# Six plain output blocks become seven-product blocks, and the branch multiplications of the short convolution move ahead

## The chip, the cores and the metric

One core of one Trainium2 chip runs the whole program in one launch. The metric is the device time of that launch in microseconds (us). TensorE (PE) multiplies matrices, VectorE (DVE) and ScalarE (ACT) do elementwise work, GpSimd (POOL) here only adds and subtracts, and SyncE (SP) issues the weight loads. All data is float32.

## The reference

The program is a small network for 256 tokens of width 1024 (D). An MLA layer and an RG-LRU layer come first. Then come two hybrid layers, called L0 and L1 in the kernel, and a last layer, called C. Only the middle of those three layers matters here:

```python
# hybrid layer (L0, L1)
y_attn = dsa_attention(q, k, v, iq, ik, iw) @ w_attn_out
y_conf = silu(layer_norm(a, conf_ln_g, conf_ln_b)) @ w_conf_out
y_sc = (c_b * causal_dwconv(c_c * c_x, sc_conv_w)) @ w_sc_out
merged = gates[:, :, 0] * y_conf + gates[:, :, 1] * y_attn + gates[:, :, 2] * y_sc
x = x + merged @ w_o
# last layer (C)
a = ret @ w_ret_out
b = moba_attention(mq, mk, mv) @ w_moba_out
mix = sigmoid(ga) * a + sigmoid(gb) * b
x = x + mix @ w_o
```

Each of `w_attn_out`, `w_ret_out` and `w_o` is a 1024 by 1024 product on 256 tokens.

## The kernel before

**Stream of weights.** All weights come from one DRAM tensor in the order of use, in blocks of up to 1 MB. SP loads them in turn into a ring of two slots. A slot is loaded again when PE has signalled its last read of it and, for a seven-product block, when POOL has finished with it too.

**Plain block.** `halves` makes 256 output columns: two column tiles, each a sum over 8 k tiles of a 128x128 weight tile with 256 tokens. With `late=2` both column tiles are first summed over 6 k tiles, and then over the last two, whose activations come later.

**Seven-product block.** `fast_block` makes the same 256 columns by a Strassen-like form. Weights, tokens and the k tiles in pairs are cut in quarters, and seven products of four k pairs each (128x128x128) take the place of eight. The form needs three other things:
- POOL makes four mixed weight tiles (`mix`): a subtraction of 1024 columns (event mix1, line 1760), then two operations of 512 columns (mix2, line 1764, and mixed, line 1767). For the first block of some stages the subtraction is cut in two of 512 columns (lines 1755 and 1757). POOL takes the blocks strictly in their order. The mixed tiles lie in two buffers, so a block is mixed once the block two before it in that stage order has been multiplied.
- DVE makes four sums s1, s2, s4, s3 of the activations (`token_sums`, lines 2237, 2239, 2241, 2242). Each of the first three waits for the one before. PE multiplies two products of plain weights and activations first (called x0 and x2 here), then the third, x1, which needs s4. After those three the slot is released. Then come four products with mixed weights (y1, y2, y3, y0).
- DVE puts the seven results together after the last product (`unite`, lines 2218 to 2227), all with one operand or more in PSUM. That also frees the PSUM banks. The blocks take two banks each out of four, in rotation, so a block needs the bank pair of the one two before it.

**The stages around the change.** In a hybrid layer, after the convolutions, PE runs four plain blocks `cb` (q = 0 to 3). `branch_b(q)` on DVE (line 2410) multiplies their results into `ys` and frees their banks. DVE does between them the layer norm's factor, `short_conv(1)`, the operands `yc` of the `conf` branch with their sums, and the top-k rounds (`ranked`). Then eight attention heads go by (`heads` on DVE, `causal_heads` on PE). Beside each PE runs one seven-product block: `conf` 0 to 3, then `sc` 0 to 3. DVE normalises a head's probabilities (line 2108) for a transpose on PE.

After the heads come two output stages of four blocks each. `attn0` is plain (`late=2`), then `attn` 0 to 2 are seven-product blocks. DVE unites each, multiplies it by its gate (line 1811, result `tmp`) and adds it to `mg` (line 2510, both inputs in SBUF). Then `o0` is plain over `mg` (`late=2`), and `o` 0 to 2 are seven-product blocks whose results go into the residual `x_res`. The sums of `mg` for `o` are made in two parts: three k pairs after the second `attn` block and the last pair after the third. The next stage, `up0`, is plain and unchanged. Layer C has the same two stages under the names `ret0`, `ret`, `o0`, `o`, after the plain `moba` blocks. Its sums of `retn` come after the multiplication of the `moba` results.

Every engine works through its own list in program order, so what is written later on DVE waits for all that stands before it.

Of the kernel before, what the change touches and what calls it, by code (L numbers as in the profile page):

```python
# [20 lines left out]
P = 128  # L21
# [40 lines left out]
def stream_plan():  # L62
# [69 lines left out]
    pl("C.ret0", "w_ret_out_3", 0, 1, 1, 8, seq(0))  # L132
    fast("C.ret", "w_ret_out_3", 0, 3, 1, lambda it, q: 256 * it + 256)
    pl("C.o0", "w_o_3", 0, 1, 1, 8, seq(0))
    fast("C.o", "w_o_3", 0, 3, 1, lambda it, q: 256 * it + 256)
# [298 lines left out]
def write_program(nc, wstream, params, consts, tokens, out, counts):  # L434
# [3 lines left out]
    with ExitStack() as ctx:  # L438
# [268 lines left out]
        def _(pe):  # L707
# [112 lines left out]

            def of_tokens(buf):

                return lambda h, k, t: buf[:, 2 * k + h, P * t:P * t + P]
# [252 lines left out]
            for l in range(2):  # L1076
# [83 lines left out]
                def branch_block(h):  # L1160
# [7 lines left out]
                halves(L + "attn0", 0, 8, [P, P], lambda k: ya[:, k, :], S, ready=[(L + "ya", h) for h in range(8)], late=2)  # L1168
                fast_stage(F, "attn", 3, 1, of_tokens(ya), (F, "ya"), None)
                halves(L + "o0", 0, 8, [P, P], lambda k: mg[:, k, :], S,  # L1170
                       ready=[(L + "attn0", "m", 0, t) for t in range(2)] + [(F, "m", k // 2) for k in range(6)], late=2)
                fast_stage(F, "o", 3, 1, of_tokens(mg), (F, "mg"), None)
# [72 lines left out]
            for h in range(4):  # L1245
                pe.wait_ge(*e.at(("C.retn", h)))
            halves("C.ret0", 0, 8, [P, P], lambda k: retn[:, k, :], S)
            fast_stage("C", "ret", 3, 1, of_tokens(retn), ("C", "retn"), None)
            halves("C.o0", 0, 8, [P, P], lambda k: mg3[:, k, :], S,
                   ready=[("C.ret0", "m", 0, t) for t in range(2)] + [("C", "m", k // 2) for k in range(6)], late=2)  # L1250
            fast_stage("C", "o", 3, 1, of_tokens(mg3), ("C", "mg"), None)
# [12 lines left out]
        def _(act):  # L1264
# [173 lines left out]
            for l in range(2):  # L1438
# [128 lines left out]
                for part in ("attn", "o"):  # L1567
                    for it in range(3):
                        first_product((F, part, it, 0))
                boundary([(L + "o0", "x", j) for j in range(2)] + [(F, "o", "x", j // 2) for j in range(6)], L + "n2", x_res, f"norm2_g_2.{l}", xg_f)  # L1570
# [104 lines left out]
            for part in ("ret", "o"):  # L1675
                for it in range(3):
                    first_product(("C", part, it, 0))
            boundary([("C.o0", "x", j) for j in range(2)] + [("C", "o", "x", j // 2) for j in range(6)], "C.n2", x_res,
# [125 lines left out]
        def _(dve):  # L1804
# [427 lines left out]
            def sum_acts(sums, lo, hi, first=0):  # L2232
# [4 lines left out]
                dve.tensor_tensor(s1, a21, a22, ALU.add).then_inc(*e.step((sums, "sum", 0)))  # L2237
                dve.wait_ge(*e.at((sums, "sum", 0)))
                dve.tensor_tensor(s2, s1, a11, ALU.subtract).then_inc(*e.step((sums, "sum", 1)))  # L2239
                dve.wait_ge(*e.at((sums, "sum", 1)))  # L2240
                dve.tensor_tensor(s4, a12, s2, ALU.subtract).then_inc(*e.step((sums, "sum", 3)))  # L2241
                dve.tensor_tensor(s3, a11, a21, ALU.subtract).then_inc(*e.step((sums, "sum", 2)))  # L2242

            def token_sums(sums, a, first=0, n=4):

                both = a[:, 2 * first:2 * first + 2 * n, 0:S].rearrange("p (k two) t -> p k two t", two=2)
                sum_acts(sums, both[:, :, 0, :], both[:, :, 1, :], first)
# [16 lines left out]
            for l in range(2):  # L2264
# [181 lines left out]
                branch_b(1)  # L2446
# [14 lines left out]
                def short_sums(h):  # L2461

                    if h > 3:
# [32 lines left out]
                heads(L, probs, lambda t: sel[:, t, 0:P * (t + 1)], branches_part, short_sums)  # L2496
                branches_part(8)
                for h in range(8):
                    dve.wait_ge(*e.at((L + "ya", h)))
                token_sums((F, "ya"), ya)  # L2500
                gated_block(L + "attn0", 0, 8, False, sg, mg)
                for t in range(2):
                    dve.wait_ge(*e.at((L + "attn0", "m", 0, t)))
                for it in range(3):
                    tiles = slice(2 * it + 2, 2 * it + 4)
                    unite((F, "attn", it, 0), both_p, 0, (F, "y", it - 1) if it else (F, "branch", 8))
                    stt(tmp[:, 0:2, 0:S], sg[:, 2 * it + 10:2 * it + 12, :], 1.0, both_p, ALU.add,
# [7 lines left out]
                for t in range(2):  # L2515
                    key = (L + "o0", 0, t)
                    dve.wait_ge(*e.at(("pe", key)))
                    b = e.bank_of(key)
                    stt(x_res[:, t, :], psum[b][:, 0:S], 0.5, x_res[:, t, :], ALU.mult,
                        ALU.add).then_inc(*e.frees(key, (L + "o0", "x", t)))  # L2520
                for it in range(3):
                    unite((F, "o", it, 0), both_p, 0, (F, "o", "x", it - 1) if it else (F, "y", 2))
                    stt(x_res[:, 2 * it + 2:2 * it + 4, :], both_p, 0.5, x_res[:, 2 * it + 2:2 * it + 4, :], ALU.mult,
# [130 lines left out]
            heads("C.", probs3, lambda t: C(f"mask{t}"), beside=retention_part)  # L2654
            for h in range(8):
# [10 lines left out]
            for h in range(4):  # L2666
                dve.wait_ge(*e.at(("C.retn", h)))
            token_sums(("C", "retn"), retn)
            gated_block("C.ret0", 0, 0, False, gab, mg3)
            for t in range(2):  # L2670
                dve.wait_ge(*e.at(("C.ret0", "m", 0, t)))
            for it in range(3):
                tiles = slice(2 * it + 2, 2 * it + 4)
                unite(("C", "ret", it, 0), both_p, 0, *([("C", "y", it - 1)] if it else []))
                stt(tmp[:, 0:2, 0:S], gab[:, 2 * it + 2:2 * it + 4, :], 1.0, both_p, ALU.add,
# [4 lines left out]
                if it == 1:  # L2680
                    token_sums(("C", "mg"), mg3, 0, 3)
            token_sums(("C", "mg"), mg3, 3, 1)
            for t in range(2):
                key = ("C.o0", 0, t)
                dve.wait_ge(*e.at(("pe", key)))
                b = e.bank_of(key)
                stt(x_res[:, t, :], psum[b][:, 0:S], 0.5, x_res[:, t, :], ALU.mult,
                    ALU.add).then_inc(*e.frees(key, ("C.o0", "x", t)))
            for it in range(3):
                unite(("C", "o", it, 0), both_p, 0, ("C", "o", "x", it - 1) if it else ("C", "y", 2))  # L2690
                stt(x_res[:, 2 * it + 2:2 * it + 4, :], both_p, 0.5, x_res[:, 2 * it + 2:2 * it + 4, :], ALU.mult,
# [70 lines left out]
```

## Time and profile before

| what | value |
|---|---|
| median of 3 runs | 1975.94 us (1975.05 to 1976.07) |
| the profiled execution, its own time | 1974.15 us |
| its span in the profile | 1972.4 us |
| PE busy | 1956.2 us (99%) |
| DVE busy | 1170.5 us (59%) |
| POOL busy | 1105.9 us (56%) |
| ACT busy | 401.9 us (20%) |
| seven-product blocks changed or added | 6 plain blocks become seven-product ones |

The span runs from the first to the last instruction of one execution. The profile records each float32 multiplication of the program as two MATMUL instructions, so a plain block is 32 records and a seven-product block 56. The ends of matmuls are modelled, so lengths are best read from the starts.

### The profile page before, as it was taken

The numbers are of one execution on the slowest core, as the hardware profiler recorded it, in microseconds if no ns is written. First come the engines' busy times: TensorE is split into PE (matmuls) and PEld (weight loads), VectorE is DVE, ScalarE is ACT, GpSimd is POOL, SyncE is SP. The second block draws the span as 40 slices with busy tenths as digits, with TensorE's granted clock in tenths as the row PEclk, the third lists the DMA queues.
The fourth block names the chain that finished last, engine by engine and source line by source line (L and its number), as shares of the span: only waits on it lengthen the run. The fifth ranks groups of instructions, "written<-read, shape, count | busy, mean of one in ns | idle before, by whom it ended". The sixth has DMA issues, their size and how long they took to land. (4 is left out here: it accounts for less than half of the span.)

```text
span 1972.4 us, 37150 instructions
## 1 busy us (share of the span) xinstructions
PE 1956.2 (99%) x14762; PEld 1847.8 (94%) x14762; DVE 1170.5 (59%) x2996; ACT 401.9 (20%) x975; POOL 1105.9 (56%) x741
## 2 busy tenths in 40 slices
PE   9999999999999999999999999999999999999999
PEld 7788889999899999999999889999999999999998
DVE  4244535989966567524888976567713377454541
ACT  2241521111221222110111222222102025220000
POOL 1000038785174587758687154578776674348773
PEclk9999999999999999999999999999999999999999
DMA  5313445443444454545444343455444442445544
GB/s 211 134 43 133 149 152 181 156 169 131 137 153 144 150 174 170 166 156 171 165 158 170 121 149 143 146 175 169 166 160 161 138 149 95 142 150 172 171 161 139
DMA packets 44266, 299.74 MB, mean 152 GB/s; under 512 B 5440, under 2 KB 6592, under 8 KB 10176
## 3 DMA queue, kind: packets, MB, share of 16 engines
q1 hardware_dynamic: 42560, 295.42, 43.7%
q8 instruction: 118, 1.93, 0.4%
q10 hardware_dynamic: 1536, 1.97, 0.3%
q14 instruction: 52, 0.43, 0.1%
HBM read 294.35 MB, written 1.05 MB: 150 GB/s over the span
## 5 line engine op out<-in xcount | busy, mean ns | idle before, releaser
L714 PE MATMUL bank<-arena,ring 128*128 128x128 f32 (+2 forms) x3878 | 615.1, 312 | 1.3 <-ACT arena L1306 0.6
L714 PEld LDWEIGHTS bank<-arena,ring 128*128 128x128 f32 x3878 | 550.3, 191 | 45.9 <-ACT arena L1306 3.1
L714 PE MATMUL bank<-xn,ring 128*128 128x128 f32 (+3 forms) x3104 | 468.3, 306 | 4.6 <-DVE arena L2410 4.6
L714 PEld LDWEIGHTS bank<-xn,ring 128*128 128x128 f32 (+1 forms) x3104 | 424.3, 191 | 36.3 <-issue 9.8
L714 PE MATMUL bank<-arena 128*128 128x128 f32 (+5 forms) x2952 | 380.3, 284 | 0.0
L714 PEld LDWEIGHTS bank<-arena 128*128 128x128 f32 (+1 forms) x2952 | 353.9, 192 | 9.3 <-issue 1.5
L714 PE MATMUL bank<-arena,h_res 128*128 128x128 f32 x2696 | 322.1, 276 | 1.9 <-POOL h_res L1764 1.2
L714 PEld LDWEIGHTS bank<-arena,h_res 128*128 128x128 f32 x2696 | 310.4, 192 | 4.8 <-POOL h_res L1764 2.4
L1760 POOL TENSOR_TENSOR arena<-ring 128x1024 f32<-128x1024 f32 (+1 forms) x100 | 235.5, 2355 | 130.2 <-DMA ring<-wstream 129.6
L1760 POOL TENSOR_TENSOR h_res<-ring 128x1024 f32<-128x1024 f32 (+1 forms) x95 | 221.6, 2333 | 113.3 <-DMA ring<-wstream 98.4
L1811 DVE SCALAR_TENSOR_TENSOR bank<-arena,par,bank 128x256 f32<-128x256 f32 x640 | 259.5, 483 | 15.3 <-DVE arena L2227 7.7
L1436 ACT ACTIVATE p1c<-bank 128x128 f32<-128x128 f32 x189 | 51.5, 273 | 731.7 <-PE bank L714 731.7
L2221 DVE TENSOR_TENSOR partial<-bank,p1c 128x128 f32<-128x128 f32 x189 | 54.3, 287 | 238.2 <-PE bank L714 238.1
L1755 POOL TENSOR_TENSOR h_res<-ring 128x512 f32<-128x512 f32 x16 | 21.6, 1350 | 239.3 <-DVE arena L2242 83.2
L1767 POOL TENSOR_TENSOR h_res<-ring,h_res 128x512 f32<-128x512 f32 (+1 forms) x111 | 144.7, 1304 | 8.7
L1764 POOL TENSOR_TENSOR h_res<-h_res,ring 128x512 f32<-128x512 f32 (+1 forms) x111 | 142.4, 1283 | 8.7
L1728 POOL TENSOR_TENSOR sq<-sq 128x256 f32<-128x256 f32 (+1 forms) x45 | 34.8, 774 | 188.6 <-ACT sq L1309 170.0
L1767 POOL TENSOR_TENSOR arena<-ring,arena 128x512 f32<-128x512 f32 (+1 forms) x100 | 129.0, 1290 | 7.8
L1764 POOL TENSOR_TENSOR arena<-arena,ring 128x512 f32<-128x512 f32 (+1 forms) x100 | 128.9, 1289 | 7.8
L2218 DVE TENSOR_TENSOR bank<-bank,p1c 128x128 f32<-128x128 f32 x77 | 22.8, 296 | 147.2 <-ACT p1c L1436 145.3
L1275 ACT ACTIVATE arena<-bank 128x256 f32<-128x256 f32 (+6 forms) x104 | 44.0, 424 | 207.0 <-PE bank L714 140.6
L714 PE MATMUL bank<-xn,h_res 128*128 128x128 f32 x648 | 84.9, 276 | 1.2 <-POOL h_res L1767 1.2
(242 smaller groups left out, 1782.5 us busy)
## 6 DMA issues: line engine op xcount, KB each, us to landing
ring<-wstream SPq DMA_DIRECT2D x264, 1024.0 KB, 4.8
ring<-wstream SPq DMA_DIRECT2D x16, 768.0 KB, 4.2
cst<-consts SPq DMA_DIRECT2D x1, 2488.0 KB, 15.0
h_res<-tokens SPq DMA_DIRECT2D x2, 544.0 KB, 5.4
arena<-arena ACTq DMA_DIRECT2D x16, 64.0 KB, 3.5
out<-arena SPq DMA_DIRECT2D x4, 256.0 KB, 5.4
arena<-arena ACTq DMA_DIRECT2D x28, 32.0 KB, 3.2
ring<-wstream SPq DMA_DIRECT2D x2, 288.0 KB, 3.5
```

Source lines behind the costliest of these rows:

```text
L714: return pe.matmul(o, lhs, rhs, start=start, stop=stop, skip_group_check=True)
L1275: ins = act.activation(dst, psum[b][0:rows, 0:T], func, **kw)
L1436: act.activation(p1c[:, b // 2 % 2, :], psum[b][:, 0:P], ACT.Copy).then_inc(*e.step((key, "p1")))
L1728: pool.tensor_tensor(out=acc, in0=acc, in1=squares[:, j, 0:T], op=ALU.add).then_inc(*e.step(event))
L1755: pool.tensor_tensor(out=m[:, 0:size], in0=w[:, size:2 * size], in1=w[:, 0:size], op=ALU.subtract).then_inc(*e.step(("mix1", block)))
L1760: pool.tensor_tensor(out=m[:, 0:2 * size], in0=w[:, size:3 * size], in1=w[:, 0:2 * size], op=ALU.subtract).then_inc(*e.step(("mix1", block)))
L1764: pool.tensor_tensor(out=m[:, 2 * size:3 * size], in0=m[:, size:2 * size], in1=w[:, 0:size], op=ALU.add).then_inc(*e.step(("mix2", block)))
L1767: pool.tensor_tensor(out=m[:, 3 * size:4 * size], in0=w[:, 3 * size:4 * size], in1=m[:, 2 * size:3 * size], op=ALU.subtract).then_inc(*e.s ...
L1811: return dve.scalar_tensor_tensor(out=out, in0=a, scalar=scalar, in1=b, op0=op0, op1=op1)
L2218: dve.tensor_tensor(view[:, 0, 0, :], x[:, 2 * P:3 * P], p1, ALU.add).then_inc(*e.step((key, "c11")))
L2221: dve.tensor_tensor(u2, y[:, 3 * P:4 * P], p1, ALU.add).then_inc(*e.step((key, "u2")))
```

## The change

All six plain first blocks (`attn0` and `o0` in L0 and L1, `ret0` and `o0` in C) become a fourth seven-product block of their stage. For `attn` and for all three `o` stages the first block is a new `late_block`: it runs all seven products over three k pairs first, and then all seven over the last pair. Each of the two rounds waits for its own part of the activations and sums. The sums of `ya` and `mg` are cut in three parts ("some": pairs 0 and 1, "most": pair 2, "sum": pair 3). In the heads, the parts of `ya` are made beside heads 6 and 7, and the last before the ninth `branches_part`. For `mg` they are made after the second, third and fourth `attn` (or `ret`) block. In C the sums of `retn` move ahead of the `moba` multiplications. In the hybrid layers `branch_b(0)` moves ahead of `short_conv(1)` and `branch_b(1)` ahead of `yc`. The number of blocks and their places in the ring stay the same.

```diff
-        pl(n + "attn0", "w_attn_out_2", l, 1, 1, 8, seq(0))
-        fast(n + "attn", "w_attn_out_2", l, 3, 1, lambda it, q: 256 * it + 256)
-        pl(n + "o0", "w_o_2", l, 1, 1, 8, seq(0))
-        fast(n + "o", "w_o_2", l, 3, 1, lambda it, q: 256 * it + 256)
+        fast(n + "attn", "w_attn_out_2", l, 4, 1, lambda it, q: 256 * it)
+        fast(n + "o", "w_o_2", l, 4, 1, lambda it, q: 256 * it)
...
+            def late_block(block, plain, sums, ready):
...
+                for ks, part, events in ((range(3), "most", ready[:-1]), (range(3, 4), "sum", ready[-1:])):
+                    for event in events:
+                        pe.wait_ge(*e.at(event))
+                    product("x", 0, w[:, 0], lambda k: plain(0, k, 0), ks, opens=True)
+                    product("x", 2, w[:, 3], lambda k: plain(1, k, 0), ks)
+                    pe.wait_ge(*e.at((sums, part, 3)))
+                    ins = product("x", 1, w[:, 2], lambda k: sums_at_k(sums, 3, k), ks)
+                    if part == "sum":
+                        ins.then_inc(*e.done(f"slot_done{slot}", ("pe", (key, "x"))))
+                    pe.wait_ge(*e.at(("mix1", block)))
+                    product("y", 1, m[:, 0], lambda k: sums_at_k(sums, 0, k), ks, opens=True)
+                    pe.wait_ge(*e.at(("mix1b", block)))
+                    pe.wait_ge(*e.at((sums, part, 2)))
+                    product("y", 2, m[:, 1], lambda k: sums_at_k(sums, 2, k), ks)
+                    pe.wait_ge(*e.at(("mix2", block)))
+                    product("y", 3, m[:, 2], lambda k: sums_at_k(sums, 1, k), ks)
+                    pe.wait_ge(*e.at(("mixed", block)))
+                    ins = product("y", 0, m[:, 3], lambda k: plain(1, k, 1), ks)
...
-                halves(L + "attn0", 0, 8, [P, P], lambda k: ya[:, k, :], S, ready=[(L + "ya", h) for h in range(8)], late=2)
-                fast_stage(F, "attn", 3, 1, of_tokens(ya), (F, "ya"), None)
...
+                late_stage(F, "attn", of_tokens(ya), (F, "ya"), [(L + "ya", h) for h in range(6)] + [(L + "ya", 7)])
+                late_stage(F, "o", of_tokens(mg), (F, "mg"), [(F, "m", it) for it in range(4)])
...
+            fast_stage("C", "ret", 4, 1, of_tokens(retn), ("C", "retn"), None)
+            late_stage("C", "o", of_tokens(mg3), ("C", "mg"), [("C", "m", it) for it in range(4)])
...
+                branch_b(0)
                 short_conv(1)
-                branch_b(0)
+                branch_b(1)
...
                 token_sums((F, "yc"), yc)
-                branch_b(1)
                 ranked(TOPK // 16, TOPK // 8)
...
+                    if h in (6, 7):
+                        for head in range(4) if h == 6 else (4, 5):
+                            dve.wait_ge(*e.at((L + "ya", head)))
+                        token_sums((F, "ya"), ya, 2 * h - 12, 8 - h, ("some", "most")[h - 6])
...
-                    if it == 1:
-                        token_sums((F, "mg"), mg, 0, 3)
+                    if it in (1, 2):
+                        token_sums((F, "mg"), mg, 2 * it - 2, 3 - it, ("some", "most")[it - 1])
                 token_sums((F, "mg"), mg, 3, 1)
```

## Rows read from the trace of the kernel before

**Rows 1.** The page: busy time of TensorE, share, instructions.
```profile
PE 1956.2 (99%) x14762; PEld 1847.8 (94%) x14762; DVE 1170.5 (59%) x2996; ACT 401.9 (20%) x975; POOL 1105.9 (56%) x741
```

**Rows 2.** TensorE's waits over the span: total us, times, longest.
```profile
PE bank L714 <- DVE arena L2410: 4.6, 2, 2.3
```

**Rows 3.** Timeline of TensorE, output stages of L0 (start, length, instructions).
```profile
611.34 9.75 PE L714 MATMUL bank<-arena,ring 128*128 128x256 f32 x56
620.93 3.74 PE L714 MATMUL bank<-arena,h_res 128*128 128x128 f32 x32
624.50 2.84 PE L714 MATMUL bank<-arena,ring 128*128 128x128 f32 x24
627.18 3.74 PE L714 MATMUL bank<-arena 128*128 128x128 f32 x32
...
637.01 9.75 PE L714 MATMUL bank<-arena,ring 128*128 128x256 f32 x56
...
662.67 2.60 PE L714 MATMUL bank<-arena,ring 128*128 128x256 f32 x11
```

**Rows 4.** Window, output stages of C: busy PE, PEld, DVE, ACT, POOL; clock.
```profile
1703.00:1754.66 51.66, 51.66 (x403) 49.96 (x402) 27.32 (x53) 4.73 (x13) 30.63 (x21) 1.00 0.52 178
```

**Rows 5.** Timeline of TensorE around the four cb blocks of L0.
```profile
516.94 13.98 PE L714 MATMUL bank<-xn,ring 128*128 128x256 f32 x64
533.26 14.05 PE L714 MATMUL bank<-xn,ring 128*128 128x256 f32 x64 [2.34 <-DVE arena L2410]
547.15 0.82 PE L714 MATMUL bank<-arena 128*128 128x128 f32 x4
```

**Rows 6.** Timeline of VectorE in the same stretch and the first two heads.
```profile
527.14 1.42 DVE L2393 TENSOR_TENSOR arena<-arena 128x256 f32<-128x256 f32 x4
...
532.70 0.74 DVE L2410 TENSOR_TENSOR arena<-bank,arena 128x256 f32<-128x256 f32 x2
...
551.13 0.53 DVE L2108 TENSOR_SCALAR arena<-arena,small 128x128 f32<-128x128 f32 x2
...
558.72 1.19 DVE L2108 TENSOR_SCALAR arena<-arena,small 128x128 f32<-128x128 f32 x2
```

**Rows 7.** Timeline of GpSimd: mix1 of the second and third conf block of L0.
```profile
552.19 2.36 POOL L1760 TENSOR_TENSOR arena<-ring 128x1024 f32<-128x1024 f32 x1 [1.03 <-DMA ring<-wstream]
...
557.22 2.35 POOL L1760 TENSOR_TENSOR h_res<-ring 128x1024 f32<-128x1024 f32 x1
```

**Rows 8.** Timeline of VectorE, from the early mg sums into o0 (L0).
```profile
634.39 0.56 DVE L2237 TENSOR_TENSOR arena<-arena 128x384 f32<-128x384 f32 x1
...
637.21 0.29 DVE L2221 TENSOR_TENSOR partial<-bank,p1c 128x128 f32<-128x128 f32 x1 [0.40 <-PE bank L714]
...
638.76 0.69 DVE L1811 SCALAR_TENSOR_TENSOR tmp<-arena,bank 128x512 f32<-128x512 f32 x1
639.48 1.01 DVE L2510 TENSOR_TENSOR arena<-arena,tmp 128x512 f32<-128x512 f32 x1
640.53 1.24 DVE L2237 TENSOR_TENSOR arena<-arena 128x128 f32<-128x128 f32 x1
641.81 1.31 DVE L2239 TENSOR_TENSOR arena<-arena 128x128 f32<-128x128 f32 x1
643.15 1.31 DVE L2241 TENSOR_TENSOR arena<-arena 128x128 f32<-128x128 f32 x1
```

**Rows 9.** Timeline of GpSimd over both output stages of L0.
```profile
611.23 1.27 POOL L1755 TENSOR_TENSOR h_res<-ring 128x512 f32<-128x512 f32 x1 [11.91 <-DMA ring<-wstream]
...
623.37 2.35 POOL L1760 TENSOR_TENSOR arena<-ring 128x1024 f32<-128x1024 f32 x1 [5.84 <-DMA ring<-wstream]
...
638.68 1.27 POOL L1755 TENSOR_TENSOR h_res<-ring 128x512 f32<-128x512 f32 x1 [4.87 <-DMA ring<-wstream]
639.91 1.72 POOL L1757 TENSOR_TENSOR h_res<-ring 128x512 f32<-128x512 f32 x1
641.71 1.26 POOL L1764 TENSOR_TENSOR h_res<-h_res,ring 128x512 f32<-128x512 f32 x1
```

More of the change, by code:

```diff
@@ L819, in fast_block, with product @@
                 return banks
+            def late_block(block, plain, sums, ready):
+                slot, key = e.next_block(), block
+                w = ring[:, slot, :].rearrange("p (s k c) -> p s k c", s=4, c=P)
+                m = mixed_of(block).rearrange("p (s k c) -> p s k c", s=4, c=P)
+                banks = {}
+                pe.wait_ge(*e.landed(slot))
+                for half in ("x", "y"):
+                    banks[half] = e.take("main", (key, half))
+                    pe.wait_ge(*e.emptied((key, half)))
+                def product(half, col, weight, act, ks, opens=False):
+                    for k in ks:
+                        ins = mm(banks[half], slice(0, P), slice(P * col, P * col + P), weight[:, k, :], act(k),
+                                 opens and k == 0, k == 3)
+                    return ins
+                for ks, part, events in ((range(3), "most", ready[:-1]), (range(3, 4), "sum", ready[-1:])):
[16 more added lines that the diff above has]
+                    ins = product("y", 0, m[:, 3], lambda k: plain(1, k, 1), ks)
+                ins.then_inc(*e.done("main_done", ("pe", (block, "t"))))
+                e.counts.events["pe", (key, "y")] = e.counts.events["pe", (block, "t")]
@@ L821, in of_tokens, with late_stage @@
+            def late_stage(L, part, plain, sums, ready):
+                late_block((L, part, 0, 0), plain, sums, ready)
+                for it in range(1, 4):
+                    fast_block((L, part, it, 0), (L, part, it, 0), plain, sums)
             def of_tokens(buf):
@@ L1567, in _ @@
                 for part in ("attn", "o"):
[L1568 removed]
+                    for it in range(4):
                         first_product((F, part, it, 0))
[L1570 removed]
+                boundary([(F, "o", "x", j // 2) for j in range(ND)], L + "n2", x_res, f"norm2_g_2.{l}", xg_f)
                 rms(L + "n2", D)
@@ L1675, in _ @@
             for part in ("ret", "o"):
-                for it in range(3):
+                for it in range(4):
                     first_product(("C", part, it, 0))
-            boundary([("C.o0", "x", j) for j in range(2)] + [("C", "o", "x", j // 2) for j in range(6)], "C.n2", x_res,
+            boundary([("C", "o", "x", j // 2) for j in range(ND)], "C.n2", x_res,
                      "norm2_w_3", xg_c)
@@ L2230, in unite, with sum_acts @@
                     dve.wait_ge(*e.at((key, part)))
-            def sum_acts(sums, lo, hi, first=0):
+            def sum_acts(sums, lo, hi, first=0, part="sum"):
                 n = lo.shape[1]
@@ L2236, in sum_acts, with token_sums @@
                 s1, s2, s3, s4 = (sums_at[sums][:, c, first:first + n] for c in range(4))
[L2237 to L2244, printed above, removed]
+                dve.tensor_tensor(s1, a21, a22, ALU.add).then_inc(*e.step((sums, part, 0)))
+                dve.wait_ge(*e.at((sums, part, 0)))
+                dve.tensor_tensor(s2, s1, a11, ALU.subtract).then_inc(*e.step((sums, part, 1)))
+                dve.wait_ge(*e.at((sums, part, 1)))
+                dve.tensor_tensor(s4, a12, s2, ALU.subtract).then_inc(*e.step((sums, part, 3)))
+                dve.tensor_tensor(s3, a11, a21, ALU.subtract).then_inc(*e.step((sums, part, 2)))
+            def token_sums(sums, a, first=0, n=4, part="sum"):
                 both = a[:, 2 * first:2 * first + 2 * n, 0:S].rearrange("p (k two) t -> p k two t", two=2)
-                sum_acts(sums, both[:, :, 0, :], both[:, :, 1, :], first)
+                sum_acts(sums, both[:, :, 0, :], both[:, :, 1, :], first, part)
             def hidden_sums(L, it, hidden):
@@ L2496, in _ @@
                 heads(L, probs, lambda t: sel[:, t, 0:P * (t + 1)], branches_part, short_sums)
+                for h in (6, 7):
+                    dve.wait_ge(*e.at((L + "ya", h)))
+                token_sums((F, "ya"), ya, 3, 1)
                 branches_part(8)
[L2498 to L2505, printed above, removed]
+                for it in range(4):
+                    tiles = slice(2 * it, 2 * it + 2)
                     unite((F, "attn", it, 0), both_p, 0, (F, "y", it - 1) if it else (F, "branch", 8))
-                    stt(tmp[:, 0:2, 0:S], sg[:, 2 * it + 10:2 * it + 12, :], 1.0, both_p, ALU.add,
+                    stt(tmp[:, 0:2, 0:S], sg[:, 2 * it + 8:2 * it + 10, :], 1.0, both_p, ALU.add,
                         ALU.mult).then_inc(*e.step((F, "y", it)))
@@ L2654, in _ @@
             heads("C.", probs3, lambda t: C(f"mask{t}"), beside=retention_part)
+            for h in range(4):
+                dve.wait_ge(*e.at(("C.retn", h)))
+            token_sums(("C", "retn"), retn)
             for h in range(8):
@@ L2679, in _ @@
                 dve.wait_ge(*e.at(("C", "m", it)))
-                if it == 1:
-                    token_sums(("C", "mg"), mg3, 0, 3)
+                if it in (1, 2):
+                    token_sums(("C", "mg"), mg3, 2 * it - 2, 3 - it, ("some", "most")[it - 1])
             token_sums(("C", "mg"), mg3, 3, 1)
[L2683 to L2691, printed above, removed]
+            for it in range(4):
+                unite(("C", "o", it, 0), both_p, 0, ("C", "o", "x", it - 1) if it else ("C", "y", 3))
+                stt(x_res[:, 2 * it:2 * it + 2, :], both_p, 0.5, x_res[:, 2 * it:2 * it + 2, :], ALU.mult,
                     ALU.add).then_inc(*e.step(("C", "o", "x", it)))
```

38 lines of the change are left out of this document (8 added, 30 removed).

## The prediction

> **What bounds the kernel now.** I read the page first: TensorE (PE) is busy for 1956.2 of 1972.4 us [rows 1], so a microsecond counts if it is taken from PE's list or from a wait of PE. The view of waits says what waits there are: only one entry belongs to a place that changes, 4.6 us in two waits of 2.3 (one in L0, one in L1) on DVE's `branch_b` [rows 2]. The timeline of PE over the output stages shows no wait at all, and the window of the same stages in C says so too: PE is busy for 51.66 of 51.66 us, at a granted clock of 1.00, while DVE has 27.3 us of work there and POOL 30.6 [rows 3, 4]. The clock can't give anything, and what the stages are worth is PE's own work minus whatever waits the new order brings. The reader should look at DVE and POOL not for their sums but for the length of single instructions, which is where I expect the result to come from.
>
> **PE's work.** From the start of `attn0` to the start of the second half of the first `attn` block are 620.93 - 611.34 = 9.59 us; that is a plain block and 24 records of 128 columns. 24 such records take 627.18 - 624.50 = 2.68 us, 0.1116 each. So a plain block takes 9.59 - 2.68 = 6.91 us and a seven-product block 56 x 0.1116 = 6.25 us (620.93 to 627.18 says the same) [rows 3]. Check: two plain and six others are 51.3 us, which is the stage [rows 3, 4]. Each exchange saves 0.66 us, six save 4.0 us. That is little: the form saves an eighth of the multiplied columns, but its records are short, and each costs more for its columns.
>
> **`branch_b` earlier.** PE starts `cb` 2 at 533.26 after a wait of 2.34 for the bank that `branch_b(0)` frees at 532.70 and after [rows 5, 6]. Moved ahead of `short_conv(1)`, it runs from 527.2, and banks are free before PE asks at 530.9: 2.34 us saved per layer. `branch_b(1)` costs DVE the same 0.74 us at its new place; `yc` comes 0.7 us later, hidden since PE asks for it only when `cb` 3 is done. But the wait doesn't all go. With PE 2.34 us earlier, `cb` 3 ends at 544.8 and the ring with it: the load of `conf` 1 lands at 549.85 instead of 552.19, where mix1 starts at once and runs 2.36 us [rows 7]. DVE isn't earlier (its list up to there is busy without a gap), so the normalisation of the first head still comes at about 550.6 (551.13 before, [rows 6]), and now under this mix1. Such an instruction does wait for POOL: in the second head the same pair, from 558.72, took 1.19 us instead of 0.53, with a POOL instruction until 559.57 [rows 6, 7]. So I take it to wait until 552.2 and end at 552.6. PE wants it at 544.8 + 0.66 + 6.25 = 551.7. That is a new wait of about 0.9 us per layer. Net 1.4 us saved per layer, 2.8 in all; bounds 0 and 2.34 per layer. The top-k's last round also falls under the mix of `conf` 0 now. No row shows a MAX8 beside POOL; if it waited like the sums below, up to the whole 2.3 us would go, which is the lower bound, and I take nothing for it, the end to which the nearest row points: an instruction with one input in SBUF and one in PSUM kept its 0.69 us beside POOL (638.76) [rows 8, 9]. [...]
>
> **What DVE's sums cost beside POOL.** This decides the case. Three instructions of 128x384 take 0.56 us each while POOL is idle (the first row of [rows 8]). Those of 128x128, a third of the size, take 1.24, 1.31 and 1.31 us at 640.53 to 643.15, beside POOL's mix of 1.72 and 1.26 us [rows 8, 9]. The ends say how: POOL's instruction from 639.91 ends at 641.63 and DVE's first at 641.77; POOL's from 641.71 ends at 642.97 and DVE's second at 643.12. DVE's instruction with both inputs in SBUF waits until the running POOL instruction ends, then takes its 0.14 us (0.54 at 512 columns), and POOL's next has begun by then, so the next DVE instruction of the chain waits for that one in turn. The same holds for the `mg` addition at 639.48, 1.01 us with POOL's 638.68 instruction ending at 639.95. Instructions with an input in PSUM keep their length (0.69 at 638.76). So under a running mix the price of a chain of sums is one POOL instruction per sum: 1.3 to 2.4 us each, not 0.3. From the last product to s4 the kernel before needs 637.01 + 0.2 to 643.15 + 1.31 = 7.3 us [rows 8], and the plain `o0` covers it: PE needs s4 only after 6.91 + 1.8 = 8.7 us.
>
> **The first `attn` block.** In the times of before: its weights now land where the plain block's did, and POOL mixes them during head 7, which is ready before 611.4. The "most" sums fit in POOL's gap before 611.2. `ya` 7 is there at about 611.9, and POOL has started the next mix at 611.23 [rows 9]; s1, s2, s4 follow its three instructions, ends at about 613.6, 615.0, 616.4, so s4 is there at 616.55. PE wants it at 611.4 + 4.69 (42 records) + 0.45 = 616.5. No loss. But the ninth `branches_part` stands behind the sums and starts at 616.8, and frees its bank at 618.1; PE wants that for the second block at 617.7. Loss 0.4, with 0.2 for the others 0.6 us per hybrid layer (bounds 0 and 1.5). In C the block is a normal one, its sums made in an empty stretch of DVE: nothing.
>
> **The first `o` block.** Nominal starts of PE's blocks after that: 618.1, 624.35, 630.6, and `o` 0 at 636.85. A slot is loaded some 5.1 us after PE's first three products: the plain block ended at 618.25, and POOL started on the next load at 623.37 [rows 3, 9]. In the late block those products end only at 616.8, so loads land at 622.0, 625.9, 632.4 and 638.3. A mix takes 5.0 us (2.4 and two of 1.3), plus what DVE holds it up, so POOL works without a gap from 622.0 to about 643.8, where before it stood still for 4.87 us until 638.68 [rows 9], since a plain block needs no mix; the three-pair sums of before lay in that gap. DVE's list now is, after the second block (end 624.35): put together and gate 3.0 us, m1 at 630.1 (POOL's 2.36 us one is in the way); four sums of "some", one POOL instruction each, to 635.8; only then the third block, whose products have been there since 630.6: 2.5 us and the addition, m2 at 639.0; four sums of "most" beside the mix of `o` 1 (638.3 to 643.8), s4 at 644.0, s3 at 644.2; then the fourth block, 3.1 us, m3 at 647.4; s4 of "sum" at 648.4 (POOL is idle by then). PE: starts at 639.0 instead of 636.85, waits again after 1.35 us until 644.0, does its five other products to 647.4, two short ones, waits until 648.4, and ends at 649.5 instead of 643.1: 6.4 us lost. Whether single races are won or lost shifts m1 and m2 by a slot of 1.3 us, but "most" ends with the mix of `o` 1 either way. Without any cover lost the bounds are 0 and 8 us per stage. In C the same count from 1703.3 gives the fourth `ret` block's end at 1728.3 and `o` 0's at 1741.0 instead of 1734.6: 6.4 again. What is queued behind: `o` 1 to 3 move as a whole, their mixes are ready, and `up0` follows as before.
>
> **Sum.** L0 and L1 each: -1.3 (two exchanges) - 1.4 + 0.6 + 6.4 = +4.3. C: -1.3 + 6.4 = +5.1. Together +13.7 us. On the profiled execution's own time, 1974.15 (span 1972.4 and 1.75 around it), that is 1987.9; the median of the runs shown is 1975.94, 1.8 higher, so I give 1988.5, between this and 1989.6.
>
> **The rivals.**
> First, the other side: the sums don't queue behind POOL. It decides if "most" is done within 1.3 us of `o` 0's start, that is, if DVE wins the lock each time or the mixes lie elsewhere. For it: DVE's 0.56 us sums at 634.39. Against it: those lie in a gap of POOL that the change fills. Then 4.0 and 4.6 us are saved and nothing lost: 1975.94 - 8.6 = 1967.3. Chance 0.13.
> Second, half of it: "some" finds a gap (mixes early by two slots), and `o` 0 loses 2 us instead of 6.4: -4.0 - 2.8 + 1.2 + 6.0 = +0.4, 1976.3. For it: POOL's stretch without a gap rests on slot times that I worked out. Chance 0.08.
> Third, worse: the waits at the heads eat all of the 2.34 us and each `o` stage loses 8: -4.0 + 1.2 + 24 = +21, 1997. Chance 0.12.
> My forecast has 0.67, with its own range of 1981 to 1994.
>
> **How the numbers follow.** Faster than by 0.2% (4 us, about what a measurement of this kernel can tell from no change) is only the first rival: 0.13. Same: 0.08. Slower: 0.67 + 0.12 = 0.79. The range of 1974 to 1996 holds the forecast, the second rival and half of the third, and leaves out 0.19.
>
> **What would show it.** In the changed kernel's profile: a plain block's 6.91 us gone and 6.25 in its place; no wait for L2410; a wait of some 0.9 us for the normalisation in the first head of L0 and L1; in front of and within the first `o` block waits of PE for DVE's sums and `mg` additions, 6 to 7 us per stage; DVE's 128x128 and 128x256 sums at 1.3 us or more each; POOL with no gap over four mixes. The prediction is wrong if those sums take 0.3 to 0.4 us, or if POOL's gap before `o` 0 survives.

## The result, and the profile after

The changed kernel takes 1987.29 us (median of 6 runs, 1984.43 to 1992.77), the kernel before beside it 1975.72 us (median of 6). The ratio is 1.0062, with a 95% interval of 1.0052 to 1.0073: 0.6% slower. The forecast was 1988.5 us. The profiled execution is the fastest of the six: 1984.43 us, span 1982.6. Its span is 10.2 us longer than that of before, while the medians are 11.6 us apart.

The page of the changed kernel, busy times. TensorE has 144 records more (6 times 24), and 2.6 us more busy time [rows 1]. The exchanges save work; the busy time rises since records behind waits ran at a lower clock (by the lengths of their rows some 4.7 us in the three stages) and since the ends of records are modelled:

```profile
span 1982.6 us, 37555 instructions
...
PE 1958.8 (99%) x14906; PEld 1853.7 (94%) x14906; DVE 1212.9 (61%) x3045; ACT 402.8 (20%) x981; POOL 1135.1 (57%) x759
```

TensorE's waits of the changed kernel (engine, line, releaser: total us, times, longest). The wait for `branch_b` [rows 2] is gone. In its place are waits for s4 of the sums (L2275) and for the `mg` additions (L2545, in C L2704), and the waits for the normalisation in a head (L2142) have grown from 1.4 us to 1.8:

```profile
PE bank L710 <- DVE arena L2275: 6.0, 4, 3.3
PE bank L710 <- DVE arena L2545: 4.3, 2, 2.3
PE bank L709 <- DVE arena L2142: 1.8, 3, 0.6
...
PE bank L710 <- DVE arena L2704: 0.9, 1, 0.9
```

Timeline of TensorE, L0: the first two heads, then the end of the `attn` stage and the first `o` block (start, length, instructions, idle time before and what ended it). The heads start 2.61 us earlier than the 547.15 of [rows 5], and the output stages at 609.45, which is 1.89 earlier than in [rows 3]:

```profile
544.54 0.82 PE L710 MATMUL bank<-arena 128*128 128x128 f32 x4
...
552.25 0.55 PE L709 MATMUL bank<-cst,arena 128*128 128x128 f32 x3 [0.64 <-DVE arena L2142]
...
609.45 2.17 PE L710 MATMUL bank<-arena,ring 128*128 128x128 f32 x18
...
631.10 3.74 PE L710 MATMUL bank<-arena 128*128 128x128 f32 x32
637.11 2.82 PE L710 MATMUL bank<-arena,ring 128*128 128x128 f32 x12 [2.27 <-DVE arena L2545]
642.06 0.94 PE L710 MATMUL bank<-arena,ring 128*128 128x128 f32 x6 [2.13 <-DVE arena L2275]
642.83 2.84 PE L710 MATMUL bank<-arena,h_res 128*128 128x128 f32 x24
...
646.31 0.49 PE L710 MATMUL bank<-arena,ring 128*128 128x128 f32 x2 [0.19 <-DVE arena L2275]
...
647.53 2.84 PE L710 MATMUL bank<-arena,ring 128*128 128x128 f32 x24
```

The block is ready to start at 634.67 (631.10 and 32 records of 0.1116). Without a wait the second `o` block would start 6.25 us later, at 640.92. It starts at 647.53: 6.6 us are lost.

Timeline of VectorE over the same time. "Some" is the 128x256 pair shown (four of them in a row), "most" is 637.00 to 640.70, "sum" begins at 645.31:

```profile
625.42 2.84 DVE L2545 TENSOR_TENSOR arena<-arena,tmp 128x512 f32<-128x512 f32 x1
628.29 1.38 DVE L2271 TENSOR_TENSOR arena<-arena 128x256 f32<-128x256 f32 x1
...
636.28 0.69 DVE L2545 TENSOR_TENSOR arena<-arena,tmp 128x512 f32<-128x512 f32 x1
637.00 2.33 DVE L2271 TENSOR_TENSOR arena<-arena 128x128 f32<-128x128 f32 x1
639.36 1.31 DVE L2273 TENSOR_TENSOR arena<-arena 128x128 f32<-128x128 f32 x1
640.70 1.30 DVE L2275 TENSOR_TENSOR arena<-arena 128x128 f32<-128x128 f32 x1
...
645.31 0.29 DVE L2271 TENSOR_TENSOR arena<-arena 128x128 f32<-128x128 f32 x1
```

Timeline of GpSimd beside it, mix of `o` 1 and the next one. It is busy from 620.02 to 641.86, in one stretch:

```profile
636.33 2.85 POOL L1794 TENSOR_TENSOR arena<-ring 128x1024 f32<-128x1024 f32 x1
639.26 1.26 POOL L1798 TENSOR_TENSOR arena<-arena,ring 128x512 f32<-128x512 f32 x1
640.60 1.26 POOL L1801 TENSOR_TENSOR arena<-ring,arena 128x512 f32<-128x512 f32 x1
652.56 2.35 POOL L1794 TENSOR_TENSOR h_res<-ring 128x1024 f32<-128x1024 f32 x1 [10.71 <-DMA ring<-wstream]
```

Read the two together. DVE's addition of 636.28 got in just before POOL's instruction of 636.33. It kept its 0.69 us, and POOL's took 2.85 us instead of 2.35. Then it turns: DVE's s1 ends at 639.33 just behind POOL's instruction (639.18), s2 at 640.67 with the next (640.52), s4 at 642.00 with the last (641.86). From 645.31 on POOL stands still, and the same sum takes 0.29 us.

The same stage in L1 loses only 4.5 us. GpSimd, VectorE and TensorE there, each in its own view of the timeline:

```profile
1248.38 2.34 POOL L1794 TENSOR_TENSOR arena<-ring 128x1024 f32<-128x1024 f32 x1 [1.24 <-DMA ring<-wstream]
```

```profile
1247.77 0.29 DVE L2271 TENSOR_TENSOR arena<-arena 128x128 f32<-128x128 f32 x1
1248.10 0.29 DVE L2273 TENSOR_TENSOR arena<-arena 128x128 f32<-128x128 f32 x1
1248.42 2.45 DVE L2275 TENSOR_TENSOR arena<-arena 128x128 f32<-128x128 f32 x1
```

```profile
1247.88 2.62 PE L710 MATMUL bank<-arena,ring 128*128 128x128 f32 x12 [2.08 <-DVE arena L2545]
1250.93 1.24 PE L710 MATMUL bank<-arena,ring 128*128 128x128 f32 x6 [0.43 <-DVE arena L2275]
```

L1 runs 610.73 us after L0 (the starts of the stage, 1220.18 and 609.45). DVE's addition stands there to 0.04 us as in L0, but the load of `o` 1's weights lands some 1.3 us later or more (L0's was there by 636.33, which is 1247.06 in the times of L1). Two of the three sums slip through the gap. What delays the load isn't shown. It is a race: in experiment eight's execution the same mix in L1 starts 0.06 us behind the addition, all three sums wait as in L0, and the block loses 6.6 us.

In C the loss is 6.3 us. TensorE there:

```profile
1739.54 1.52 PE L710 MATMUL bank<-arena,ring 128*128 128x128 f32 x6 [3.29 <-DVE arena L2275]
1740.85 3.93 PE L710 MATMUL bank<-arena,h_res 128*128 128x128 f32 x24
1744.62 0.83 PE L710 MATMUL bank<-arena,ring 128*128 128x128 f32 x6
```

The 24 records take 3.93 us instead of 2.84, and the six before them take 1.31 us from start to start instead of 0.67. That is 1.7 us of this loss, and it isn't a wait. The windows of the changed kernel (length; busy PE, PEld, DVE, ACT, POOL; clock, DMA share, GB/s) say what it is. TensorE's granted clock fell behind the waits. The first row is L0 between the two waits: 0.50, where the output stages of L0 had 1.00 before (from 611.34 to 662.67). The other two are whole first `o` blocks, of L0 and of C:

```profile
637.90:640.00 2.10, 2.03 (x10) 1.73 (x9) 2.07 (x2) 0.00 (x0) 2.02 (x2) 0.50 0.00 0
634.00:650.00 16.00, 11.41 (x87) 10.76 (x86) 14.12 (x28) 0.28 (x1) 7.62 (x5) 0.89 0.22 76
...
1725.00:1745.00 20.00, 15.84 (x125) 15.49 (x125) 18.19 (x26) 0.28 (x1) 15.34 (x10) 0.91 0.31 106
```

**Where the 10.2 us of the span come from**, by starts of stages: up to the output stages of L0 -1.9 us; those stages +5.5 (56.84 us instead of 51.33); from there up to those of L1 -2.1; there +3.65; between L1 and C +0.1; output stages of C +5.0.

### The profile page after: what moved, and what is told of

It is laid out like the page before. It is cut to its first block and busy times, and to the rows that moved or that the text cites. A ratio compares the mean times of both kernels' runs of the same rounds, so it can differ in the third digit from the quotient of the medians.

```text
span 1982.6 us, 37555 instructions
## 1 busy us (share of the span) xinstructions
PE 1958.8 (99%) x14906; PEld 1853.7 (94%) x14906; DVE 1212.9 (61%) x3045; ACT 402.8 (20%) x981; POOL 1135.1 (57%) x759
## 5 line engine op out<-in xcount | busy, mean ns | idle before, releaser
L710 PE MATMUL bank<-arena,ring 128*128 128x128 f32 (+2 forms) x3830 | 596.4, 309 | 12.8 <-DVE arena L2275 6.0
L710 PEld LDWEIGHTS bank<-arena,ring 128*128 128x128 f32 x3830 | 534.0, 192 | 54.3 <-DVE arena L2275 7.0
L710 PE MATMUL bank<-arena 128*128 128x128 f32 (+4 forms) x3144 | 402.7, 284 | 0.0
L710 PEld LDWEIGHTS bank<-arena 128*128 128x128 f32 (+1 forms) x3144 | 375.8, 192 | 9.3 <-issue 1.5
L1794 POOL TENSOR_TENSOR arena<-ring 128x1024 f32<-128x1024 f32 (+1 forms) x106 | 250.1, 2359 | 110.0 <-DMA ring<-wstream 109.4
L1798 POOL TENSOR_TENSOR arena<-arena,ring 128x512 f32<-128x512 f32 (+1 forms) x106 | 138.0, 1302 | 8.3
L1801 POOL TENSOR_TENSOR arena<-ring,arena 128x512 f32<-128x512 f32 (+1 forms) x106 | 136.4, 1287 | 8.3
L2257 DVE TENSOR_TENSOR partial<-bank,partial 128x256 f32<-128x256 f32 x195 | 82.8, 424 | 6.7
```

What stands on the lines that cost most here:

```text
L710: return pe.matmul(o, lhs, rhs, start=start, stop=stop, skip_group_check=True)
L1794: pool.tensor_tensor(out=m[:, 0:2 * size], in0=w[:, size:3 * size], in1=w[:, 0:2 * size], op=ALU.subtract).then_inc(*e.step(("mix1", block)))
L1798: pool.tensor_tensor(out=m[:, 2 * size:3 * size], in0=m[:, size:2 * size], in1=w[:, 0:size], op=ALU.add).then_inc(*e.step(("mix2", block)))
L1801: pool.tensor_tensor(out=m[:, 3 * size:4 * size], in0=w[:, 3 * size:4 * size], in1=m[:, 2 * size:3 * size], op=ALU.subtract).then_inc(*e.s ...
L2257: dve.tensor_tensor(partial[:, 1:3, :], y[:, P:3 * P].rearrange("p (n t) -> p n t", t=P), partial[:, 0:1, :].broadcast_to([P, 2, P]), ALU. ...
```

## The experiments

The kernel before ran beside each set of runs: 1975.93 us beside experiments one to four, 1975.58 beside five to eight, 1974.73 beside nine. The changed kernel's 1987.29 us is from the set of the result, so a difference between medians of two sets is good to about 1 us.

**One. The kernel before, with only the two branch multiplications moved.**

```diff
+                branch_b(0)
                 short_conv(1)
-                branch_b(0)
+                branch_b(1)
...
-                branch_b(1)
                 ranked(TOPK // 16, TOPK // 8)
```

> The kernel before with only the branch multiplications moved ahead. Theory (the wait of 2.34 us per hybrid layer goes, about 0.6 us of it comes back as a wait for the first head's normalisation under GpSimd's mix): two layers save 1.9 to 2.0 each, so 3.5 to 4.7 us faster than before. Rival (VectorE stays as late as it was and the heads give all of it back): within 1 us of before.

Measured: 1971.4 us (8 runs) against 1975.93, ratio 0.9975 [0.9965, 0.9986]; span 1969.3, clock 1.0. The largest of TensorE's waits; L2410 no longer appears among them:

```profile
PE bank L713 <- DVE arena L2108: 2.7, 4, 0.9
```

The heads of L0 start at 544.90, `attn0` at 609.80, 1.5 us earlier than before. The medians give 4.5 us, the spans 3.1. Part of the 4.5 is clock: all eight runs of this kernel have a mean granted clock of 1.0, but only five of the 13 of before, with a median of 1973.97 us; the other eight, at 0.998 and 0.999, have 1977.06. Against the five the gain is 2.6 us. Where before loses its clock in those runs isn't shown; the two waits that are gone here are the likely place. The multiplications alone make the kernel faster, and the rest of the change costs more than it seemed: some 16 us between this kernel and the changed one.

**Two. The changed kernel with the first `attn` (`ret`) block plain again, `o` left exchanged.**

```diff
-        fast(n + "attn", "w_attn_out_2", l, 4, 1, lambda it, q: 256 * it)
+        pl(n + "attn0", "w_attn_out_2", l, 1, 1, 8, seq(0))
+        fast(n + "attn", "w_attn_out_2", l, 3, 1, lambda it, q: 256 * it + 256)
...
```

> The changed kernel with attn and ret back to a plain first block; the three o stages stay exchanged. Theory (the exchanged o block itself shortens the cover, whatever stands before it): 4 us and 2 us saved, about 5 to 6.5 us lost per o stage: 9 to 14 us slower than before. Rival (late slot of the first attn block is the cause): o loses 2 us or less per stage, and the time is at or below before.

Measured: 1990.15 us (4 runs), ratio 1.0066 [1.0051, 1.0081]; span 1988.8, clock 0.997. With +14.2 us against before it lies just above what was expected. TensorE waits 11.8 us in all for s4 here, in six waits. The first `o` block of L0 is ready to start at 634.3 and the second starts at 648.46, so 7.9 us are lost in it. The exchange of `attn` isn't to blame: with it plain, the first `o` blocks lose as much and more (7.9, 6.5 and 6.5 us in L0, L1 and C, against 6.6, 4.5 and 6.3).

**Three. The changed kernel with the first `o` block plain again, `attn` left exchanged.**

```diff
-        fast(n + "o", "w_o_2", l, 4, 1, lambda it, q: 256 * it)
+        pl(n + "o0", "w_o_2", l, 1, 1, 8, seq(0))
+        fast(n + "o", "w_o_2", l, 3, 1, lambda it, q: 256 * it + 256)
...
```

> The changed kernel with the three o stages back to a plain first block; attn and ret stay exchanged. Theory (the loss sits in the first o block alone, since a plain one covers VectorE's sums): about 4 us saved by the branch multiplications, 2.0 by three exchanges, 1.2 lost at the first attn blocks: 4 to 6 us faster than before. Rival (the late slot of the first attn block, and GpSimd without a gap after it, are enough to make any first o block wait): some waits of 2 us or more remain at o, time within 2 us of before or slower.

Measured: 1970.21 us (6 runs), ratio 0.9969 [0.9957, 0.9981]; span 1969.4, clock 1.0. TensorE goes from the last `attn` block into the plain one without a wait:

```profile
631.48 3.74 PE L712 MATMUL bank<-arena 128*128 128x128 f32 x32
635.05 9.75 PE L712 MATMUL bank<-arena,ring 128*128 128x256 f32 x56
```

The three `o` exchanges cost 17.1 us by the medians (1987.29 - 1970.21) and 13.2 by the spans, and they are the whole loss. Without them the change makes the kernel 5.7 us faster than before. Nearly all of that is experiment one's: the three `attn` and `ret` exchanges add 1.2 us by the medians and nothing by the spans (1969.4 against 1969.3).

**Four. The changed kernel with GpSimd's mixes of four blocks a layer cut down to 8 columns.**

```diff
+                def cut(t, a, b):
+
+                    return t[:, a * size:a * size + (8 if block in few else (b - a) * size)]
...
```

> The changed kernel, but GpSimd mixes only 8 columns instead of all per instruction in four blocks of each layer (attn or ret 2 and 3, o 0 and 1), so the weights of the last four products there are stale; everything else runs as in the changed kernel. Theory (VectorE's two-SBUF-input additions wait for GpSimd's instructions one by one): sums of 128x128 take 0.3 us, the waits at the first o block nearly vanish, 5 to 8 us faster than before. Rival (VectorE's order is the cause, the third block is put together only after the sums of the second): waits of several us at o remain, time near the changed kernel's, 8 to 12 us slower than before.

Measured: 1968.5 us (4 runs), ratio 0.9961 [0.9946, 0.9976]; span 1965.6, clock 1.0. This kernel leaves out most of the mixed weights, so its result can't be used. The order of VectorE's list is that of the changed kernel, and its instructions are those too. Timeline of VectorE, an `mg` addition and the first sums of "some" and "most":

```profile
624.25 0.69 DVE L2551 TENSOR_TENSOR arena<-arena,tmp 128x512 f32<-128x512 f32 x1
624.98 0.43 DVE L2277 TENSOR_TENSOR arena<-arena 128x256 f32<-128x256 f32 x1
...
631.23 0.29 DVE L2277 TENSOR_TENSOR arena<-arena 128x128 f32<-128x128 f32 x1
```

Nothing but GpSimd's instructions was made short, and 2.84, 1.38 and 2.33 us became 0.69, 0.43 and 0.29. TensorE has no wait in the first `o` block (634.29 to 640.54, 6.25 us), nor in those of L1 and C. Against experiment one, which has the plain blocks, the span is 3.7 us shorter (1965.6 against 1969.3): nearly the 4.0 us of six exchanges. The rival, that DVE's list is too long or wrongly ordered for the form, is refuted: the same list is in time when nothing runs beside it.

**Five. The changed kernel with the gated product kept in PSUM**, so that the `mg` addition has one input in SBUF; the sums still have two.

```diff
-                    stt(tmp[:, 0:2, 0:S], sg[:, 2 * it + 8:2 * it + 10, :], 1.0, both_p, ALU.add,
+                    stt(both_p, sg[:, 2 * it + 8:2 * it + 10, :], 1.0, both_p, ALU.add,
...
-                    dve.tensor_tensor(mg[:, tiles, :], mg[:, tiles, :], tmp[:, 0:2, 0:S], ALU.add)
+                    dve.tensor_tensor(mg[:, tiles, :], mg[:, tiles, :], both_p, ALU.add)
...
```

> The changed kernel with the gated product left in PSUM instead of tmp, so that the addition to mg has one input in PSUM and one in SBUF. Theory (only an instruction with two SBUF inputs waits for GpSimd): the additions take 0.69 us instead of up to 2.84 under a mix, the chain of sums starts up to 2.3 us earlier, the first o block loses 1.5 to 4 us instead of 4.5 to 6.6: 1977 to 1983. Rival (any VectorE instruction that reads SBUF waits for GpSimd): the additions still take up to 2.8 us, time as the changed kernel, 1984 to 1990.

Measured: 1978.19 us (10 runs), ratio 1.0014 [1.0004, 1.0023]; span 1976.7. That is 9.1 us less than the changed kernel. Timeline of VectorE: the addition of the second block, and behind it the first sum.

```profile
625.07 0.69 DVE L2545 TENSOR_TENSOR arena<-arena,bank 128x512 f32<-128x512 f32 x1
625.79 1.92 DVE L2271 TENSOR_TENSOR arena<-arena 128x256 f32<-128x256 f32 x1
```

Timeline of GpSimd, the one instruction beside both:

```profile
625.07 2.36 POOL L1794 TENSOR_TENSOR arena<-ring 128x1024 f32<-128x1024 f32 x1
```

Under the same GpSimd instruction the addition with an operand in PSUM takes 0.69 us, and GpSimd's keeps its 2.36, though both began at 625.07; the sum with two in SBUF lasts until 627.7. In these rows it is where the operands lie that counts, not that both engines are busy.

**Six. The changed kernel, GpSimd holds the mix of `o` 1 until the last `mg` sums are made.**

```diff
+                if block[1:] == ("o", 1, 0):
+                    pool.wait_ge(*e.at(((block[0], "mg"), "sum", 2)))
```

> The changed kernel, with GpSimd made to wait with the mix of the second o block until VectorE has made the last sums of mg; all else and the result are the same. Theory (the most sums queue behind that mix): those sums take 0.3 us each, the first o block loses about 2.4 us instead of 4.5 to 6.6, the held mix is still in time for TensorE; 7 to 12 us faster than the changed kernel, 1975 to 1980. Rival (GpSimd is the resource that is short, so a held mix makes the second o block wait): no gain over the changed kernel, 1985 or more, with waits of TensorE on GpSimd.

Measured: 1976.7 us (10 runs), ratio 1.0008 [0.9998, 1.0017]; span 1975.1. 10.6 us less than the changed kernel. TensorE has one wait left in this block, for an addition, and the second `o` block starts at 642.75:

```profile
636.39 2.25 PE L710 MATMUL bank<-arena,ring 128*128 128x128 f32 x18 [2.06 <-DVE arena L2547]
```

"Most" takes 0.29 us a sum here (from 636.28). The late mix costs nothing in L0: TensorE meets it ready.

**Seven. Both mends together**, the diffs of experiments five and six in one kernel.

> Both of these: additions to mg from PSUM, and the mix of the second o block held. Theory: the first o block loses about 1 us, so all eight moves together give -4 -4 +1.2 +3: 1970 to 1973, no better than the changed kernel with plain first o blocks. Rival (gains of the two overlap, since both free the same wait): 1976 or more.

Measured: 1971.44 us (11 runs), ratio 0.9981 [0.9972, 0.9990]; span 1969.1, clock 1.0. The first `o` block of L0 loses 1.0 us:

```profile
634.00 1.50 PE L710 MATMUL bank<-arena,ring 128*128 128x128 f32 x12
635.77 0.94 PE L710 MATMUL bank<-arena,ring 128*128 128x128 f32 x6 [0.26 <-DVE arena L2277]
...
641.24 2.84 PE L710 MATMUL bank<-arena,ring 128*128 128x128 f32 x24
```

The first `o` blocks of L1 and C lose 1.2 and 0.8. So with VectorE and GpSimd kept apart the kernel with all six exchanges is 4.1 us faster than before. But that is what experiment one gives without a single exchange: 1971.44 us here against 1971.40 there, spans 1969.1 and 1969.3. Of the 4.0 us that the exchanges save in TensorE's work, 3.0 are still lost in the three first `o` blocks. Against the version with plain `o` blocks (1970.21, from another set of runs) there is no gain either.

**Eight. The changed kernel with matmuls to fill TensorE's waits**: 4 and 7 more of 128x256 in the two waits of each first `o` block, whose results nothing reads.

```diff
+        FILL = (4, 7)
...
+                fill(FILL[0])
...
+                    if part == "most":
+                        fill(FILL[1])
                     pe.wait_ge(*e.at((sums, part, 3)))
```

> The changed kernel with 4 multiplications of 128x256 before the first o block and 7 after its first two products, whose results nobody reads, so that TensorE is not idle in the two waits. Theory A (the waits also cost clock: in the changed kernel 12 records after the first wait took 2.7 instead of 1.3 us at a granted clock of 0.5): the granted clock stays at 1.00, 2 to 4 us faster in the median and a smaller spread, 1983 to 1985. Theory B (the clock falls only inside the waits and costs nothing): same as the changed kernel, within 1 us, or slower by what the added work runs over.

Measured: 1985.63 us (4 runs, 1984.77 to 1985.89), ratio 1.0054 [1.0038, 1.0069]; span 1983.0. The windows over the three first `o` blocks show the clock at full:

```profile
630.00:650.00 20.00, 19.23 (x147) 17.96 (x147) 18.11 (x31) 0.55 (x2) 11.84 (x8) 1.00 0.25 81
1236.00:1258.00 22.00, 20.95 (x162) 19.68 (x162) 20.25 (x28) 0.56 (x2) 15.66 (x10) 1.00 0.28 96
1728.00:1750.00 22.00, 21.88 (x176) 21.11 (x174) 19.14 (x33) 0.83 (x3) 13.65 (x10) 1.00 0.36 127
```

The median is 1.7 us lower than the changed kernel's, which is neither of the two expectations: theory A asked for 2 to 4 us, theory B for 1 us at most. The runs lie within 1.1 us, where the changed kernel's lie within 8.3. The fastest runs are equal (1984.77 and 1984.43). In the two profiled executions the first `o` blocks lose 6.3, 6.6 and 5.1 us here and 6.6, 4.5 and 6.3 there, so what C gains is used up in L1, where the race for the sums went the other way. Four runs are few, so how much of the median and of the spread comes from the clock is argued and not shown. That the clock doesn't fall here, where TensorE has work in the waits, is shown, in this execution and by a mean clock of 1.0 in all four runs.

**Nine. Plain `o` blocks and the product in PSUM**, the diffs of experiments three and five in one kernel.

> The changed kernel with the first block of each o stage plain again (as in the run before that did only this, 1970.2 us) and with the gated product kept in PSUM, so that the mg addition has one input in SBUF instead of two. Question: whether the two mends add up. Theory A (in the version with the plain o blocks PE has no wait left at the o stages, so a shorter mg addition is hidden): 1970 to 1971 us, same as without the PSUM addition. Rival (the additions still held back something, such as the clock or the second attn block): 1966 to 1969 us. Mg additions with an input in PSUM are expected at 0.69 us beside GpSimd's mixes.

Measured: 1969.93 us (10 runs) against 1974.73, ratio 0.9975 [0.9966, 0.9985]; span 1967.9, clock 1.0. The same as experiment three within what can be told. The additions take 0.69 us, but TensorE already didn't wait for them there. The plain first `o` block had cover for everything behind it.

## Why the prediction was right

**TensorE's work.** Where nothing waits, the seven-product block takes 6.25 us from start to start (622.17 to 628.42), as forecast. Experiment four, with GpSimd's mixes cut short, shows it in the late form too. The -4.0 us for six exchanges stand.

**`branch_b` earlier.** The wait went, and a smaller one came: 0.64 us for the normalisation in the first head instead of the forecast 0.9. The pair of instructions did stand waiting for GpSimd's mix1 (2.04 us from 550.15, where it took 0.53 before [rows 6]). But that mix started at 549.50 and not at 549.85, and so the pair ended at 552.19 and not at 552.6. Net 1.9 us in L0 and 2.1 in L1 instead of 1.4; alone, 1.5 in L0. The bound taken at nothing held: the top-k's MAX8 beside GpSimd's mix kept its length, 0.41 us. Timeline of the changed kernel, VectorE and then GpSimd:

```profile
543.28 0.41 DVE L2457 MAX8 decay<-arena 128x8 f32<-128x256 f32 x1
```

```profile
542.95 1.27 POOL L1789 TENSOR_TENSOR h_res<-ring 128x512 f32<-128x512 f32 x1 [34.29 <-issue]
```

Timeline of VectorE before, at the same place; GpSimd did nothing there until 545.32:

```profile
543.31 0.41 DVE L2423 MAX8 decay<-arena 128x8 f32<-128x256 f32 x1
```

**Sums beside GpSimd.** The mechanism and its price were right: 1.3 to 2.4 us per sum, one GpSimd instruction each, except for two sums in L1. Experiments four, five and six each take all or part of it away in another manner (shorter mixes, an operand elsewhere, another time) and each gives back 9 to 19 us.

**The first `attn` block.** Forecast 0.6 us lost per hybrid layer, measured 0.2 in L0 and 0.5 in L1.

**The first `o` block.** In L0 the count was right step by step, but for one thing that cost nothing: the 12 records between the two waits took 2.8 us and not 1.35, at a granted clock of 0.50, and still ended before s4 was there. In the times of before (1.89 us added) s4 of "most" was ready at 643.9 (forecast 644.0), m3 at 647.2 (647.4), s4 of "sum" at 648.1 (648.4), the start of the second block at 649.4 (649.5). Loss 6.6 against 6.4. In L1 the sentence "'most' ends with the mix of `o` 1 either way" failed: it has the mix start before the sums do, and there its weights landed after two of them. 4.5 us were lost. In C 6.3 us were lost, close to the forecast by luck: 1.7 us of it are the fallen clock, and the waits proper are 4.6.

**The clock.** "The clock can't give anything" was right for what the change saves in the profiled execution, though not in all runs of before (experiment one), and wrong for what it brings. I read 1.00 in the stage of before [rows 4], where TensorE never waited, and carried it over to a stage with waits of 2 to 3 us. The term was missing: 1.7 us in C and 0.4 in L1 in the profiled execution (there six records take 1.08 us from start to start instead of 0.67).

**The sum.** Forecast for the profile +13.7, measured +10.2. The difference of 3.5 is L1's `o` stage with its first `attn` block (2.05), `branch_b` (1.2), and 0.1 to 0.2 each in L0 and C. The forecast of 1988.5 lies only 1.2 us above the measured median because two misses stand against each other. For the profiled execution the forecast was 1987.9 and the measured time 1984.43, 3.4 us less. But I added 0.6 us for the distance from there to the median, and this kernel's is 2.9 (1987.29 - 1984.43). That they meet is luck, and a forecast as close as this says less for the working than L0's steps do.

## What to carry to other kernels

Before giving an engine a new chain of small dependent instructions, look at what the neighbouring engine runs at that time: here a sum with both inputs in SBUF waited for the end of the GpSimd instruction beside it, so that a chain of three was paid with 4 to 5 us instead of 0.9 (128x128) or 1.3 (128x256). A plain block that saves no multiplication may be the cover under which such a chain is hidden; six exchanges saved 4.0 us of TensorE's work, and three of them took 17 by the medians, since that cover went with them. When a cheap part of a change (two calls moved, 4.5 us faster) travels with an expensive one, time them one by one: no complete version with exchanges is more than 1.5 us faster than the two moved calls alone.

## What the runs showed of the hardware

TensorE's granted clock fell in the output stages, which were at 1.00 before, where TensorE waited there. After waits of 2.27 us in L0 (idle from 634.8 to 637.1) it was at 0.50 from 637.9 to 640.0, and after one of 3.29 us in C 24 records took 3.93 us instead of 2.84. But not every such wait was followed by it. After the 2.34 us wait of the kernel before [rows 5] the next records kept their length (64 of 128x256 in 14.05 us there, 13.98 without a wait). In experiment six the clock stayed at 1.00 after a wait of 2.06 us in L0, and after one of 2.10 us in L1, the only one in that block, it was at 0.50 from 1245.6 to 1247.5. What decides isn't shown. With matmuls in the waits (experiment eight) it stayed at 1.00 over the three first `o` blocks.

In L0 the exclusion beside GpSimd went both ways: a VectorE addition that began 0.05 us before GpSimd's instruction kept its 0.69 us, and the GpSimd instruction took 2.85 us instead of 2.35.
